# GpSimd instead of VectorE makes the low pieces of the normalised rows for the gather

## The reference

```
mix = hybrid_mixer(h)                                   # attention, spatial gating, conv module, w_out
h   = LayerNorm(alpha * h + mix) * g + b
scores = sigmoid(h @ w_router)                          # 16 experts in 4 groups
pick the best group, then its 2 best experts; gates = normalised scores
out = sum over experts e of gates[:, e] * (silu(h @ w_gate[e]) * (h @ w_up[e])) @ w_down[e]
h   = LayerNorm(alpha * h + out) * g + b
```

## Time and profile before

| | |
|---|---|
| median of 3 runs | 698.88 us (697.13 to 699.33) |
| the profiled execution's own time | 698.79 us |
| its span, from the first to the last instruction | 697.0 us |
| busy: PE, DVE, ACT, POOL | 659.8, 319.6, 167.1, 71.4 us |
| mean granted TensorE clock | 0.98 |

### The profile page before, as it was taken

One profiled execution on the slowest core, in us unless ns is written; L12 is line 12 of the kernel. 1 busy time (PEld: TensorE's weight loads), 2 busy tenths in 40 slices (PEclk: granted clock), 3 DMA queues, 4 the chain that ended last, 5 costly groups with the idle time before them and its releaser, 6 DMA issues.

```text
span 697.0 us, 7595 instructions
## 1 busy us (share of the span) xinstructions
PE 659.8 (95%) x3087; PEld 342.1 (49%) x3087; DVE 319.6 (46%) x613; ACT 167.1 (24%) x324; POOL 71.4 (10%) x67
## 2 busy tenths in 40 slices
PE   7999999999999999998689999989999999999982
PEld 4874587543333543332278656856333345333330
DVE  6898867610322220320687978773220330320326
ACT  3411763231110311110153128424101113101100
POOL 3403100510000000000060040006000000000001
PEclk9999999999999999999879999999999999999996
DMA  8999836099999999999999953334999999999991
GB/s 282 367 391 414 372 123 241 13 371 395 430 428 428 428 429 427 428 422 420 394 381 403 414 228 121 122 121 194 361 420 431 427 426 430 424 432 423 420 375 63
DMA packets 39438, 240.74 MB, mean 345 GB/s; under 512 B 4508, under 2 KB 8932, under 8 KB 24036
## 3 DMA queue, kind: packets, MB, share of 16 engines
q1 hardware_dynamic: 36612, 236.49, 83.7%
q10 hardware_dynamic: 2784, 3.67, 1.5%
HBM read 239.10 MB, written 1.05 MB: 345 GB/s over the span
## 4 chain that ended last, share of the span: by engine, by line
PE 73%; DVE 11%; DMA 10%; ACT 2%; issue 2%; SPq 1%; POOL 0%; DVEq 0%; POOLq 0%; ACTq 0%
PE bank L586 22%; PE bank L619 10%; DMA ring<-in_w_up 8%; PE bank L490 8%; PE bank L504 6%; PE bank L564 5%; PE bank L601 5%; PE bank L634 4%; PE bank L654 4%; DVE mix L1435 4%; PE bank L696 2%; DMA ring<-in_w_in 2%; DVE in_lo L1212 2%; PE bank L609 1%; PE bank L768 1%
## 5 line engine op out<-in xcount | busy, mean ns | idle before, releaser
L586 PE MATMUL bank<-ring,xe 128*64 128x512 f32 x768 | 167.6, 593 | 0.1
L1372 DVE TENSOR_TENSOR area_b<-area_b,bank 128x512 f32<-128x512 f32 x16 | 11.0, 688 | 231.4 <-PE bank L586 167.0
L586 PEld LDWEIGHTS bank<-ring,xe 128*64 128x64 f32 x768 | 55.2, 137 | 108.3 <-issue 107.7
L619 PE MATMUL bank<-ring,area_b 128*64 128x512 f32 x384 | 85.0, 596 | 0.0
L1392 DVE SCALAR_TENSOR_TENSOR y_lo<-bank,slot_gate,y_hi 128x512 fp32r<-128x512 f32 x32 | 24.0, 751 | 89.4 <-ACT y_hi L959 89.4
L1060 POOL TENSOR_TENSOR rstd<-var_eps,half_neg 128x1 f32<-128x1 f32 x18 | 11.8, 659 | 512.4 <-DVE var_eps L1159 512.3
L601 PE MATMUL bank<-ring,xe 128*64 128x512 f32 x256 | 57.0, 596 | 3.7 <-DMA ring<-in_w_up 2.6
L490 PE MATMUL bank<-ring,xT_area 128*128 128x512 f32 x128 | 55.9, 593 | 0.0
L619 PEld LDWEIGHTS bank<-ring,area_b 128*64 128x64 f32 x384 | 26.5, 137 | 50.0 <-issue 50.0
L1435 DVE SCALAR_TENSOR_TENSOR mix<-mix,tapsT 128x256 f32<-128x256 f32 x120 | 49.9, 486 | 0.0
L959 ACT ACTIVATE y_hi<-bank,slot_gate 128x512 fp32r<-128x512 f32 x32 | 22.0, 687 | 98.4 <-PE bank L619 70.7
(11 more groups left out here) (171 smaller groups left out, 859.4 us busy)
## 6 DMA issues: line engine op xcount, KB each, us to landing
ring<-in_w_gate SPq DMA_DIRECT2D x32, 2048.0 KB, 20.0
ring<-in_w_up SPq DMA_DIRECT2D x32, 2048.0 KB, 19.6
ring<-in_w_down SPq DMA_DIRECT2D x32, 2048.0 KB, 21.0
ring<-in_w_in SPq DMA_DIRECT2D x9, 2048.0 KB, 18.1
ring<-in_w_out SPq DMA_DIRECT2D x4, 2048.0 KB, 21.0
ring<-in_w_in SPq DMA_DIRECT2D x2, 1024.0 KB, 7.7
h<-in_x SPq DMA_DIRECT2D x2, 512.0 KB, 4.1
ln_par<-in_ln_mix_g ACTq DMA_DIRECT2D x2, 512.0 KB, 14.7
```

The lines of the kernel that those rows point to most:

```text
L586: mm = pe.matmul(bank[2 + m][e * SLOTS:(e + 1) * SLOTS, :], xe[:, k, at + e * SLOTS:at + (e + 1) * SLOTS], w[e][:, k * DE:(k + 1) * DE], s ...
L619: mm = pe.matmul(bank[5 + n][e * SLOTS:(e + 1) * SLOTS, :], hidT[:, k, e * SLOTS:(e + 1) * SLOTS], w[e][:, k * D + n * BANK:k * D + (n + 1 ...
```

## The change

The subtraction `n_lo = normal - n_hi` leaves VectorE's program and enters GpSimd's, behind the third `inverse_deviations(TB)` and ahead of the wait for `pick`. Shapes, operands and both semaphores stay; there are two such instructions per layer, four in all. No DMA is added or moved.

```
@@ gpsimd
                 inverse_deviations(TB)
                 inverse_deviations(TB)
                 inverse_deviations(TB)
+                for b in range(TB):
+                    pool.wait_ge(n_hi_ready, TB * l + b + 1)
+                    pool.tensor_tensor(n_lo[:, b, :], normal[:, b, :], n_hi[:, b, :].bitcast(F32), ALU.subtract)\
+                        .then_inc(n_lo_ready, 1)
                 pool.wait_ge(main_sems["pick"], TB * (ITERS * l + 1))
@@ vector
-            def normal_low(l, b):
-                dve.wait_ge(n_hi_ready, TB * l + b + 1)
-                dve.tensor_tensor(n_lo[:, b, :], normal[:, b, :], n_hi[:, b, :].bitcast(F32), ALU.subtract)\
-                   .then_inc(n_lo_ready, 1)
@@ vector, end of the mixer
                     norm_center(i, h[:, b, :], b)
-                normal_low(l, 0)
                 half_turned(l, 1)
-                normal_low(l, 1)
                 routing(l)
```

## The result

The changed kernel takes 704.39 us (median of 8 runs, 703.09 to 708.09), the kernel before in the same runs 698.37 us (696.72 to 699.33). The ratio is 1.0098, with a 95% interval of 1.0075 to 1.0121: slower by about 6 us, where 706.9 had been predicted. The profiled execution of the changed kernel took 705.35 us, its span is 703.6 us (before: 698.79 and 697.0).

What follows compares the result with a forecast made beforehand. Bound by TensorE and the expert weights, with delays between output projection and gather reaching the end one to one. Removal 0, addition 0, collision 4.1 and clock 3.9 summed to 8.0 us more, giving 706.9; range 699.5 to 710.

Steps and rivals of the forecast that it cites:

- The removal: Four subtractions of 1.22 us leave VectorE, hidden by TensorE's turn and the exponential; gain 0.
- The addition: Two GpSimd subtractions per layer, taken as 2.38 us each, done before the gather needs them; cost 0 by itself.
- The collision: GpSimd's first subtraction holds up VectorE's L1173 of block 1; turn 1.9 us late in layer 0, 2.2 in layer 1.
- The sign that L1173 would end 0.1 to 0.2 before or after GpSimd's end: Expected in the changed profile for L1173 of block 1, lengthened to about 3.0 us instead of 0.81.
- GpSimd's margin at the routing: GpSimd's second subtraction lets go of SBUF before VectorE's L1267 comes; margin 0.5 us, cost 0.
- The race: GpSimd's subtraction and VectorE's L1173 reach for SBUF together behind block 1's power; GpSimd was taken to win.
- The clock: TensorE's longer idle time before block 1's turn lowers its clock from 2.4 to 1.2 GHz; 3.9 us together.
- the middle, 1.95 per layer: Price taken for the lowered TensorE clock, between 0 and 3.9 us per layer, in both layers.
- The upper bound of 3.9 per layer: Most a lowered clock could cost: turn 0.8 us, L821 0.6, the 18 products 2.5.
- Collision without the clock: Rival: L1173 is held up but TensorE's clock stays at 1.00; 703.0 us, chance 0.18.
- VectorE first: Rival: L1173 gets SBUF first, GpSimd's later end delays L1267 by 0.3 and 0.5 us; 699.7 us, chance 0.16.
- The gate that the ring of weights puts on the end: Weight transfers restart at a fixed distance behind the gather, so delay before it reaches the end one to one.

Runs made afterwards that it cites:

- experiment 2: Kernel before, GpSimd making only block 0's subtraction, behind L1173 of block 1, VectorE still making block 1's; 698.48 us against 698.43.
- experiments 1 and 8: Changed kernel with GpSimd's subtractions waiting for VectorE's normalised block 1 (700.13 us), and with twelve one-column GpSimd fills ahead of the subtractions instead (698.32 us).
- experiment 3: Changed kernel with eight filler products for TensorE in its hole, behind the strips of block 0; 701.39 us against 698.43.
- run with four fills: Changed kernel with four one-column fills of a spare tile between GpSimd's power of block 1 and its subtractions; 708.20 us against 698.48.
- e4_extra_beside: Kernel before, VectorE making both pieces, plus one extra GpSimd subtraction per layer where the change puts it; 705.23 us against 698.43.
- experiment 5: Changed kernel with each of GpSimd's subtractions cut into four of 256 columns; 698.19 us against 698.48.

## Why the prediction was right

**The removal, 0.** Right as far as tested: experiment 2 takes one subtraction off VectorE in each layer, and the time is the same.

**The addition, 0 by itself.** GpSimd's instruction takes 2.35 us (2.38 taken). Moved away from L1173 (experiments 1 and 8), all four together cost 1.0 to 1.2 us, nearly all of it at the routing's first instruction (with the fills, 0.1 in layer 1 is that of the longer L1180); in the changed kernel the second one of layer 0 ends at 125.84, before L1271 at 126.18, of layer 1 at 469.12, before 470.26, and costs nothing.

**The collision, 4.1.** Right: 3.8 measured (experiment 3), 1.75 and 2.02 for 1.9 and 2.2. VectorE's instruction was let in 0.26 us before GpSimd's end, not 0.13, and GpSimd's was 0.03 shorter. The sign that L1173 would end 0.1 to 0.2 before or after GpSimd's end was wrong, and not what my own working gave: 122.42 against 121.74 there, 0.55 behind it here. GpSimd's margin at the routing was 0.3 us in layer 0 and 1.1 in layer 1, for 0.5.

The race came out as I read it from the power at 347.84, but not for the reason that I gave. "Some tens of nanoseconds" was too narrow: GpSimd still wins when its record begins 0.06 us behind VectorE's. The Trainium skill (SBUF — State Buffer, section "Who interferes with whom") says that between GpSimd and a VectorE instruction in a two-port mode whichever issues first keeps the shared ports for its whole instruction and blocks the other fully. No run here shows which mode L1177 is in. The blocking is what its 2.83 us show, and, with the order turned, GpSimd's 2.81 us in the run with twelve fills. That the first to issue wins can't be read from recorded starts: by those VectorE was first in the run with four fills, and lost.

**The clock, 3.9: the term that was mis-sized.** Of the 2.5 us by which 706.9 is above 704.39 it has most. I took "the middle, 1.95 per layer", for two layers. In the profiled execution the clock fell in layer 1 only and cost 2.2 us there (4.25 - 2.02), so the price of a fall was about right and the number of falls, in the executions that can be looked at, was not. How the 2.2 came about is not quite as I had it, though. The fall came late in the turn, which lost 0.12 of my 0.8; L821 and L826, the products behind it, lost 0.65 together, against my 0.6 for L821 alone; the 18 products lost 1.74 of my 2.5, and 1.47 of it passed on. (Half of the 3.68 us of 16 transposes is 1.84, not my 1.94; the turn of layer 1 in the run with four fills took 1.81.) "In layer 1 more surely than in layer 0" was right: of the profiled executions with the full collision and without added products, three have a fall in layer 1 alone (705.35, 705.69 and e4_extra_beside), and the one with four fills (709.48) has both. The upper bound of 3.9 per layer was reached once, in layer 1 of the run with four fills.

"The clock to fall in most executions" can't be told from the totals. The 14 runs of the changed kernel lie in steps: six at 703.0 to 703.6, three at 705.2 to 705.7, five at 706.6 to 708.4. It is tempting to read them as no fall, one and two, but the profiles speak against it. e4_extra_beside has a fall and took 703.07, because its border of the layers was 2.3 us shorter than the changed kernel's (328.45 against 330.78); e3_clock_held has none and took 703.05, with a border of 330.70. With the clock held, four of seven runs lie under 701.5; of the 14 none does. So perhaps all 14 had at least one fall; that is argued, not seen. How near the median came to 706.9 is therefore luck in part: it hangs on which step the middle run lies in.

With the collision's 3.8 and the profiled 2.2 the sum is 6.0, the 5.98 of the stretches; 0.78 at the border, which no step of mine had and whose cause is not shown, and -0.2 behind it make the 6.6 of the spans.

**The rivals.** Collision without the clock (703.0): no profile of the changed kernel shows it. e3_clock_held is that case, brought about by fillers, and took 701.39. That some of the six runs near 703 were of this sort is not excluded. VectorE first (699.7, 0.3 + 0.5 at the routing) is what the run with twelve fills is: +0.34 and +0.62 in the stretches, 1.0009 in the ratio, no measurable change. The gate that the ring of weights puts on the end, one to one, held as well: transfers and end are late by what the gathers are.

## What to carry over

Before work goes from VectorE to GpSimd because VectorE is the busier, ask which of VectorE's instructions from SBUF to SBUF start while it runs, and who waits for those: a piece of 2.35 us that nobody waited for cost 1.75 and 2.02 us where it began just ahead of one on the path. Start it behind that instruction, which left 1.7 us of the 6 here, or cut it, as experiment 5 did, which left nothing measurable; neither gained anything, because what was taken off VectorE had not been on the path. The hole of 2.15 us in front of TensorE cost as much again by the clock, and the one of 1.69 nothing. Look at how often the clock falls, not only at what one fall costs, and look in profiles: the runs of one kernel can lie in steps for more than one reason.

## What was not expected of the hardware

- GpSimd's 128x1024 subtraction held VectorE's instruction although its record begins 0.06 us later (119.86 against 119.80); at 0.33 us later it did not.
- VectorE's 0.81 us of work on L1173's 1024 columns began 0.25 to 0.27 us before the recorded end of GpSimd's instruction, in all kernels with the collision, and between pieces of 256 columns after 0.4 us. Even a VectorE instruction of 0.18 us on 128x32 elements is held: 0.53 to 0.92. Counted back in the same way, that one began 0.13 to 0.15 before GpSimd's end, as L1346 did in the kernel before, so there is no one figure for all.
- Idle time of TensorE in front of the turn: 1.69 us in layer 0 kept the clock, 2.15 in layer 1 lost it, in both profiled executions of the changed kernel; with four fills 1.83 and 2.29 both lost it. Whether the same hole can do either is not shown. At 0.50, or partly so, the same 18 products took 5.78 to 6.93 us instead of 4.04, L821 1.08 instead of 0.65.
- At the border of the layers TensorE's 64 products of L696 take 15.74 us in the kernel before and 14.05 to 17.08 in the others without added products there, depending on when the clock comes back up. The timeline of the changed kernel and that of e4_extra_beside:

```profile
356.84 15.98 PE L696 MATMUL bank<-xT_area,ring 128*128 128x256 f32 x64 [1.50 <-ACT xT_area L864]
```

```profile
356.48 14.05 PE L696 MATMUL bank<-xT_area,ring 128*128 128x256 f32 x64 [1.51 <-ACT xT_area L864]
```

In the first the clock is 0.50 until 358 and 0.66 from 358 to 362, in the second 1.00 from 358. That scatters the totals of the kernels here by some 2 us, and may be why some ratios lie below what their stretches add up to; for each single total it is argued, not shown.
